# Three unused tiles in front of the split weights, HH and the attention tiles of a two-block float32 kernel

## The chip, the cores and the metric

The kernel runs on one core of a Trainium2 chip. The metric is the device time of one execution in microseconds (us). A profiled execution has a time of its own, from its first to its last instruction, the span.

## The reference

Two blocks act on x of 512 tokens by 1,024 channels, all in float32:

```python
# first block
z = rmsnorm(h, g_mix) @ w_in + b_in                       # 1024 -> 1536
y = concat(conformer_conv_group(a, gate, ...), multiscale_pool_group(p, ...))
h = h + y @ w_out
h = h + (silu(n @ w_gate) * (n @ w_up)) @ w_down          # n = rmsnorm(h, g_ffn); 1024 -> 2816 -> 1024
x = rmsnorm(h, g_final)
# second block: layer 0 has 16 forgetting heads of 64, layer 1 has 8 differential heads
for layer in range(2):
    h = attention(x)                                      # fox, then diff with rope and a shared K, V
    x = layer_norm(ALPHA * x + h)
    f = (silu(g) * val) @ ffn_w_out                       # g, val: x @ ffn_w_in after a causal conv of width 3
    x = layer_norm(ALPHA * x + f)
```

The convolution of the first block is depthwise, 31 taps over 512 channels.

## The kernel before

Every tile has 128 partitions; an activation is held turned, channels on the partitions and the 512 tokens along the row. A float32 product is made of three matmuls on halves of the numbers: each operand is split into a high part in fp32r (XH, WH) and what is left over (XL, WL), and `product` adds WH by XL, WH by XH and WL by XH into one PSUM bank (lines 982 to 984). The weight tile is the stationary operand, 128 by 128; the moving operand is 128 by 512, or by 256 where a stage is worked in halves of the tokens.

The weights come in items of up to 8 tiles. SP's queue copies an item into `raw` (2 slots), ScalarE makes WH of it (line 1604) and GpSimd WL (line 741); WH and WL have 4 slots of 8 tiles of 128 floats each. TensorE waits for a half item's WL (`step`, line 980 and before) and goes through its k tiles. STAGES lists the order of the items: in, out, gu0, down0, qkv1, out1, gu1, down1, qkv2, out2, gu2, down2. The moving operand is XH and XL in the in, gu and qkv stages, HH and HL (the hidden layer, 22 tiles) in the down stages, OH and OL in the out stages after attention. In qkv1 and qkv2 the weight items are woven with the score, softmax and value steps of the heads that came before; those read tiles of the attention group (PTH, PTL, VX, QX, KX and others). The first two items of a stage and the last two are worked in halves of 256 tokens, so that the norm between the stages can overlap them (lines 1055, 1067, 1068, and `half_item`).

The convolution is done on TensorE too: `conv_pairs` (line 1282 on) takes for each pair m of taps 128 weight columns from dg_h and dg_l, and as moving operand 256 floats of u_h and u_l that start at float m. So the moving start goes 4 bytes on with each of the 16 values of m; a row of u_h for one group is 271 floats (1,084 bytes) long, and there are two groups g.

SBUF is laid out by order of allocation. `sb(name, shape, dtype, stack)` takes the next free bytes of every partition, in steps of 32 bytes, and a stack that is closed gives its bytes back, so the tiles allocated next lie over it. From the start of a partition: xres (16,384 bytes); XH and XL (16,384 each), and over them, since `wide` is closed, yout and last_rows; raw (8,192); WH and WL (16,384 each); par (3,072), ones (512), identr (512), masks (1,024), work (12,288), small (432). Then three groups start at the same byte and lie over each other: `first` (xin, upad, dg_h, u_h and more of the first block), `ffn` (HH, HL of 45,056 bytes each, act_g, hid) and `att` (PTH, PTL, OH, OL, OF, pmap, and in it either the tiles of the first or those of the second kind of attention). The functions that use the tiles are the same in both kernels:

```python
            def product(out_, wh, wl, xh, xl, start, stop):
                pe.matmul(out_, wh, xl, start=start, stop=False)
                pe.matmul(out_, wh, xh, start=False, stop=False)
                return pe.matmul(out_, wl, xh, start=False, stop=stop)
```

Of the kernel before, what the change touches and what calls it, by code (L numbers as in the profile page):

```python
# [26 lines left out]
P = 128  # L27
# [170 lines left out]
def two_blocks(nc, A, out):  # L198
    ctx = ExitStack()
    with ctx:  # L200
        def sb(name, shape, dt=F32, stack=None):
            return (stack or ctx).enter_context(nc.sbuf_tensor(name, shape, dt))
# [7 lines left out]
        def sems(name, n):  # L210
# [8 lines left out]
        yout = sb("yout", [P, 2 * QT, S])  # L219
        last_rows = sb("last_rows", [P, DT, S])  # L220
        raw = sb("raw", [P, RAW, DT, P])
        WH = sb("WH", [P, SLOTS, DT, P], F32R)
        WL = sb("WL", [P, SLOTS, DT, P], F32R)
        par = sb("par", [P, 6 * P])
# [39 lines left out]
        icnt = sb("icnt", [P, PAD], stack=first)  # L264
        first.close()
        ffn = ExitStack()
        HH = sb("HH", [P, FT, S], F32R, stack=ffn)
        HL = sb("HL", [P, FT, S], F32R, stack=ffn)
        act_g = sb("act_g", [P, 2, S], stack=ffn)
        hid = sb("hid", [P, 2, S], stack=ffn)  # L270
        ffn.close()
        att = ExitStack()
        PTH = sb("PTH", [P, 2, QT * KEYS + S - P], F32R, stack=att)
        PTL = sb("PTL", [P, 2, QT * KEYS + S - P], F32R, stack=att)
        OH = sb("OH", [P, DT, S], F32R, stack=att)
# [7 lines left out]
        wf, wf_h, wf_l = (x.rearrange("p (k h) -> p k h", h=FOX_HEADS)  # L283
                          for x in (pmap[:, 0, 0:DT * FOX_HEADS], PTH[:, 0, 0:DT * FOX_HEADS], PTL[:, 0, 0:DT * FOX_HEADS]))
        QX = sb("QX", [P, 2, 2, S], F32R, stack=fox)
# [8 lines left out]
        QZ = sb("QZ", [P, 2, 2, S], F32R, stack=dif)  # L294
        KD = PTH[:, 1, 0:2 * S].rearrange("p (c s) -> p c s", c=2)
        QL = PTL[:, 1, 0:S]
# [153 lines left out]
        def down_part(i):  # L450

            t, j = divmod(i, 4)
            sizes = LAST_DOWN if t == DT - 1 else DOWN
            return sum(sizes[:j]), sizes[j]

        def half_of_maps(x, h):

            return x.rearrange("p k (m h c) -> p k m h c", m=2, h=2)[:, :, :, h, :]

        def maps_of_half(x, h):  # L460

            return x.rearrange("p k (h m c) -> p k h m c", h=2, m=2)[:, :, h, :, :]
# [5 lines left out]
        def halves(kt):  # L468

            return slice(0, kt - kt // 2), slice(kt - kt // 2, kt)  # L470
# [9 lines left out]
        def keys_of(x, head, i):  # L480

            return x[:, head, i * P:i * P + (i + 1) * KEYS].rearrange("p (j s) -> p j s", s=KEYS)[:, :, 0:P]
# [245 lines left out]
        def _(pool):  # L728
            own = Chain(pool, gv)

            def low(g, kt=DT, turned=False, of=range(2), count=1):

                s = g.slot(SLOTS)
                for half in of:
                    ks = halves(kt)[half]
                    wl, x, wh = WL[:, s, ks, :], raw[:, g.slot(RAW), ks, :], WH[:, s, ks, :].bitcast(F32)
                    if turned:
                        wl, x, wh = (maps_of_half(WL[:, s], half), half_of_maps(raw[:, g.slot(RAW)], half),
                                     maps_of_half(WH[:, s].bitcast(F32), half))
                    pool.wait_ge(w_hi, g.times(2).n(half + 1) if len(of) == 2 else count)  # L740
# [119 lines left out]
            def lows_of_hidden(name, layer):  # L860
                with pool.Fori(0, FT // 2) as it:
                    for j in range(2):
                        low(Nth(STAGES[name][0] + 2 * j + 3, it, 4))
                        if layer:
# [3 lines left out]
                        pool.tensor_tensor(HL[:, bass.ds(it * 2 + j, 1), :], hid[:, j:j + 1, :],  # L868
                                           HH[:, bass.ds(it * 2 + j, 1), :].bitcast(F32), ALU.subtract).then_inc(h_lo[j], 1)
                        if not layer:  # L870
# [109 lines left out]
        def _(pe):  # L980
# [5 lines that stand above are left out]
            def step(g, b, hi, lo, k0, k, kt, start, stop, turned=False):  # L986
# [3 lines left out]
                if k == kt - kt // 2 and not turned:  # L990
                    pe.wait_ge(w_lo, g.times(2).n(2))
                s = g.slot(SLOTS)
                mm = product(banks[b][:, :], WH[:, s, k, :], WL[:, s, k, :], hi[:, k0 + k, :], lo[:, k0 + k, :],
                             start and k == 0, stop and k == kt - 1)
# [3 lines left out]
            def item(g, b, hi, lo, k0, kt, start, stop):  # L998

                for k in range(kt):  # L1000
                    step(g, b, hi, lo, k0, k, kt, start, stop)
# [29 lines left out]
            def half_item(name, i, b, hi, lo, k0, kt, h, a=0, z=None, first=True, last=True):  # L1031

                g = STAGES[name][0] + i
                c = slice(h * HALF, (h + 1) * HALF)
                s = g % SLOTS
                for k in range(a, kt if z is None else z):
                    if h == 0 and k == 0:
                        pe.wait_ge(w_lo, 2 * g + 1)
                    if h == 0 and k == kt - kt // 2:
                        pe.wait_ge(w_lo, 2 * g + 2)  # L1040
                    mm = product(halves_of[h][b][:, 0:HALF], WH[:, s, k, :], WL[:, s, k, :], hi[:, k0 + k, c], lo[:, k0 + k, c],
                                 first and k == 0, last and k == kt - 1)
                return mm

            def stage_in_halves(name, m):
# [3 lines left out]
                for h in range(2):  # L1049
                    c = slice(h * HALF, (h + 1) * HALF)  # L1050

                    def by_low(k):
                        pe.wait_ge(x_lo, DT + half_tile(m, h, k) + 1)
                        for j in range(2):
                            mm = pe.matmul(bank[(u + j) % 2][:, c], WH[:, (g + j) % SLOTS, k, :], XL[:, k, c],  # L1055
                                           start=False, stop=k == DT - 1)
# [3 lines left out]
                    for k in range(DT):  # L1060
                        pe.wait_ge(x_top, half_tile(m, h, k) + 1)
                        for j in range(2):
# [3 lines left out]
                            s = (g + j) % SLOTS  # L1066
                            pe.matmul(bank[(u + j) % 2][:, c], WH[:, s, k, :], XH[:, k, c], start=k == 0, stop=False)  # L1067
                            pe.matmul(bank[(u + j) % 2][:, c], WL[:, s, k, :], XH[:, k, c], start=False, stop=False)  # L1068
# [27 lines left out]
            def down(name, layer):  # L1096
# [5 lines left out]
                def tile(t, it=0):  # L1102
                    u = Nth(STAGES[name][1] + t, it, 2)
                    bank_free(u)
                    for j in range(4):
                        if t == 0 and j == 3:
                            for q in h_lo:
                                pe.wait_ge(q, (layer + 1) * FT // 2 + OPEN)
                        item(Nth(STAGES[name][0] + 4 * t + j, it, 8), u.slot(2), HH, HL, *down_part(j), j == 0, j == 3)

# [12 lines left out]
                def part(j, h, a=0, z=None):  # L1123
                    i = 4 * (DT - 1) + j
                    return half_item(name, i, 1, HH, HL, *down_part(i), h, a, z, j == 0, j == 3)

# [299 lines left out]
            def attend(e, slot, turn):  # L1426
                pe.wait_ge(o_read[e], turn.n() + OPEN)
                for j in range(QT):
                    mm = product(ob[e][:, j * P:], VH[:, slot, j * P:(j + 1) * P], VL[:, slot, j * P:(j + 1) * P],
                                 *(x[:, e, j * (KEYS + P):j * KEYS + S] for x in (PTH, PTL)), j == 0, j == QT - 1)  # L1430
                mm.then_inc(o_done[e], 1)

            def attend_folded(e, slot, turn):

                pe.wait_ge(o_read[e], turn.n() + OPEN)
                for j in range(QT):
                    v = VX[:, slot, (2 * j + e) * P:(2 * j + e + 1) * P]
                    for x in (PTL, PTH):
                        mm = pe.matmul(ob[e][:, j * P:], v, x[:, e, j * (KEYS + P):j * KEYS + S], start=j == 0 and x is PTL,  # L1439
                                       stop=j == QT - 1 and x is PTH)  # L1440
                mm.then_inc(o_done[e], 1)
# [148 lines left out]
        def _(act):  # L1590
# [226 lines left out]
            def hidden_hi(it, j, name):  # L1817

                act.wait_ge(bank_read[1], Nth(STAGES[name][1] + 2 * j + 1, it, 4).round(2, 1))
                act.activation(HH[:, bass.ds(it * 2 + j, 1), :], hid[:, j:j + 1, :], ACT.Copy).then_inc(h_hi, 1)  # L1820

# [41 lines left out]
            def map_hi(b, used, head, i):  # L1863
                act.wait_ge(t_done[b], used.n(1))
                act.activation(keys_of(PTH, head, i),
                               tb[b][:, 0:(i + 1) * P].rearrange("p (j q) -> p j q", q=P), ACT.Copy).then_inc(pt_h[b], 1)
# [77 lines left out]
            def conv_hidden(name, layer):  # L1944
# [3 lines left out]
                def hidden(it, j):  # L1948
# [14 lines left out]
                    act.wait_ge(hid_ready[j], Nth(FT * (layer - 1) + j, it, 2).round(2, 1) + OPEN)  # L1963
                    act.activation(HH[:, bass.ds(it * 2 + j, 1), :], hid[:, j:j + 1, :], ACT.Copy).then_inc(h_hi, 1)

# [717 lines left out]
```

## Time and profile before

| what | value |
|---|---|
| time, median of 2 runs | 1817.22 us (1816.87 to 1817.57) |
| profiled execution, span | 1818.9 us |
| TensorE busy | 1774.2 us, 98% of the span, 8,755 matmuls |
| GpSimd busy | 1029.9 us, 57% |
| ScalarE busy | 795.8 us, 44% |
| VectorE busy | 765.2 us, 42% |
| granted TensorE clock, mean | 0.991 |

PE is TensorE's matmuls, PEld its weight loads, DVE VectorE, ACT ScalarE, POOL GpSimd. Matmuls are pipelined: a row gives the time that one is in flight, and the next one starts before it ends. The pace of a stretch is therefore read from the starts of its rows, or from the count of matmuls in a window.

### The profile page before, as it was taken

To read this page: it belongs to the slowest core of one execution; us is meant where nothing else is said; L and a number is where in the kernel's file an instruction comes from. 1 tells how busy PE (TensorE), PEld (TensorE's weight loads), DVE (VectorE), ACT (ScalarE), POOL (GpSimd) and SP (SyncE) were. 2 spreads that over 40 slices of the span, in tenths; PEclk is the share of its full clock that TensorE was granted. 3 is DMA by queue.
4 is the path that set the end of the run, shared out by engine and by line. 5 is a ranking of instruction groups with operands and counts; after the bars stand their busy time and mean duration, and the time that the engine had idled before them with its cause. 6 is when DMAs were issued, how large, how long until landed. Compare 5 with 4: busy or idle time off the path is not lost.

```text
span 1818.9 us, 26859 instructions
## 1 busy us (share of the span) xinstructions
PE 1774.2 (98%) x8755; PEld 1477.6 (81%) x8755; DVE 765.2 (42%) x1382; ACT 795.8 (44%) x1674; POOL 1029.9 (57%) x926
## 2 busy tenths in 40 slices
PE   8999999999999999999999999999999999999997
PEld 6879888888887888788888888877777888888886
DVE  7963000001235556553333322487875533333224
ACT  5644323322245555464444422555565644444231
POOL 7856555555462333466666655555554666666551
PEclk9999999999999999999999999999999999999999
DMA  5312333323334454323333233333332233332332
GB/s 153 92 47 82 104 92 92 101 87 103 91 90 115 123 133 122 86 73 99 102 92 94 85 104 87 82 94 81 87 77 79 63 111 93 96 100 78 104 91 97
DMA packets 327253, 171.94 MB, mean 95 GB/s; under 512 B 43459, under 2 KB 316949, under 8 KB 327189
## 3 DMA queue, kind: packets, MB, share of 16 engines
q1 hardware_dynamic: 327172, 171.12, 33.8%
q8 instruction: 35, 0.57, 0.1%
q14 instruction: 30, 0.24, 0.0%
q10 hardware_dynamic: 16, 0.00, 0.0%
HBM read 152.15 MB, written 2.10 MB: 85 GB/s over the span
## 4 chain that ended last, share of the span: by engine, by line
PE 87%; DVE 5%; POOL 3%; ACT 2%; issue 1%; DMA 1%; SPq 0%; DVEq 0%; ACTq 0%; POOLq 0%
PE bank L982 24%; PE bank L984 24%; PE bank L983 24%; PE attended L982 2%; PE attended L983 2%; PE attended L984 2%; PE turned L1423 1%; POOL WL L741 1%; PE attended L1439 1%; PE bank L1055 1%; PE bank L1067 1%; POOL psums L804 1%; PE bank L1068 1%; DVE small L2453 0%; PE score L1406 0%
## 5 line engine op out<-in xcount | busy, mean ns | idle before, releaser
L741 POOL TENSOR_TENSOR WL<-raw,WH 128x512 fp32r<-128x512 f32 (+3 forms) x656 | 774.8, 1203 | 555.6 <-ACT WH L1604 553.1
L982 PE MATMUL bank<-XL,WH 128*128 128x512 f32 x1432 | 568.8, 397 | 3.7 <-DVE work L2576 1.2
L984 PE MATMUL bank<-XH,WL 128*128 128x512 f32 x1432 | 557.8, 390 | 0.0
L983 PE MATMUL bank<-XH,WH 128*128 128x512 f32 x1432 | 557.4, 389 | 0.0
L1604 ACT ACTIVATE WH<-raw 128x512 fp32r<-128x512 f32 (+3 forms) x656 | 338.5, 565 | 307.7 <-PE bank L984 190.9
L984 PEld LDWEIGHTS bank<-XH,WL 128*128 128x128 f32 x1432 | 269.7, 188 | 56.8
L982 PEld LDWEIGHTS bank<-XL,WH 128*128 128x128 f32 x1432 | 270.1, 189 | 55.6 <-DVE work L2576 1.5
L983 PEld LDWEIGHTS bank<-XH,WH 128*128 128x128 f32 x1432 | 270.4, 189 | 49.9
L982 PE MATMUL bank<-HL,WH 128*128 128x512 f32 (+1 forms) x528 | 200.6, 380 | 0.0
L983 PE MATMUL bank<-HH,WH 128*128 128x512 f32 (+1 forms) x528 | 200.3, 379 | 0.0
L984 PE MATMUL bank<-HH,WL 128*128 128x512 f32 (+1 forms) x528 | 200.3, 379 | 0.0
L2365 DVE SCALAR_TENSOR_TENSOR xres<-xres,bank 128x512 f32 (+1 forms) x27 | 18.5, 687 | 260.4 <-PE bank L984 257.7
L868 POOL TENSOR_TENSOR HL<-hid,HH 128x512 f32 x66 | 85.1, 1289 | 70.5 <-ACT HH L1820 70.5
L982 PEld LDWEIGHTS bank<-HL,WH 128*128 128x128 f32 x528 | 98.8, 187 | 21.5
L984 PEld LDWEIGHTS bank<-HH,WL 128*128 128x128 f32 x528 | 98.8, 187 | 21.5
L983 PEld LDWEIGHTS bank<-HH,WH 128*128 128x128 f32 x528 | 98.8, 187 | 21.3
L1860 ACT ACTIVATE pmap<-score,small 128x128 f32<-128x128 f32 (+3 forms) x128 | 67.2, 525 | 102.8 <-DVE small L2453 102.6
L2427 DVE TENSOR_TENSOR hid<-bank,act_g 128x512 f32<-128x512 f32 x21 | 14.5, 692 | 207.5 <-PE bank L984 203.9
L1958 ACT ACTIVATE hid<-bank,par 128x512 f32<-128x512 f32 x42 | 32.7, 778 | 143.6 <-PE bank L984 143.6
L2513 DVE SCALAR_TENSOR_TENSOR hid<-bank,par,hid 128x511 f32<-128x511 f32 x42 | 31.5, 750 | 150.7 <-ACT hid L1958 150.5
L2513 DVE SCALAR_TENSOR_TENSOR act_g<-bank,par,act_g 128x511 f32<-128x511 f32 x42 | 31.5, 750 | 133.8 <-ACT act_g L1958 133.8
L2453 DVE TENSOR_REDUCE small<-score 128x1 f32<-128x128 f32 (+3 forms) x128 | 62.1, 486 | 34.6 <-PE score L1408 23.3
(366 smaller groups left out, 2532.0 us busy)
## 6 DMA issues: line engine op xcount, KB each, us to landing
raw<-in_ffn_w_in SPq DMA_DIRECT2D x88, 512.0 KB, 3.8
raw<-in_w_gate SPq DMA_DIRECT2D x22, 512.0 KB, 3.8
raw<-in_w_up SPq DMA_DIRECT2D x22, 512.0 KB, 3.9
raw<-in_ffn_w_out SPq DMA_DIRECT2D x28, 384.0 KB, 3.3
raw<-in_ffn_w_out SPq DMA_DIRECT2D x28, 320.0 KB, 3.2
raw<-in_a_w_in SPq DMA_DIRECT2D x16, 512.0 KB, 4.2
raw<-in_kv_w SPq DMA_DIRECT2D x32, 256.0 KB, 3.2
raw<-in_w_in SPq DMA_DIRECT2D x12, 512.0 KB, 3.8
```

The source lines that it names most:

```text
L741: pool.tensor_tensor(wl, x, wh, ALU.subtract).then_inc(w_lo, 1)
L804: own.link(pool.tensor_tensor(dst[:, PAD:], src[:, PAD:], src[:, PAD - d:PAD + S - d], ALU.add))
L868: pool.tensor_tensor(HL[:, bass.ds(it * 2 + j, 1), :], hid[:, j:j + 1, :], HH[:, bass.ds(it * 2 + j, 1), :].bitcast(F32), ALU.subtract).th ...
L982: pe.matmul(out_, wh, xl, start=start, stop=False)
L983: pe.matmul(out_, wh, xh, start=False, stop=False)
L984: return pe.matmul(out_, wl, xh, start=False, stop=stop)
L1604: act.activation(wh, x, ACT.Copy).then_inc(w_hi, 1)
L1860: act.activation(pmap[:, n % 4, 0:k], sc[c][:, 0:k], ACT.Exp, bias=small[:, n % 4:n % 4 + 1], accum_out=small[:, 4 + n % 4:5 + n % 4]).the ...
L1958: act.activation(dst[:, j, :], ff_banks(it, j)[side][:, :], ACT.Identity, bias=ff_par(layer - 1, 3, n), scale=ff_par(layer - 1, 2, n)).the ...
L2365: dve.scalar_tensor_tensor(out=r, in0=r, scalar=factor, in1=src[j][:, :].rearrange("p (a s) -> p a s", a=1), op0=ALU.mult, op1=ALU.add).th ...
L2453: dve.tensor_reduce(small[:, n % 4:n % 4 + 1], sc[c][:, 0:(n // 2 + 1) * P], AX_X, ALU.max, negate=True).then_inc(mx[c], 1)
L2513: own.link(dve.scalar_tensor_tensor(out=dst[:, j, 1:], in0=src[:, 0:S - 1], scalar=ff_par(layer - 1, 1, n), in1=dst[:, j, 1:], op0=ALU.mul ...
```

## The change

Three tiles are allocated that nothing reads or writes: 56 floats (224 bytes) in front of WH, 40 floats (160 bytes) at the start of the `ffn` group in front of HH, and 32 floats (128 bytes) at the start of the `att` group in front of PTH. All that is allocated after a gap in the same group moves on by its size; a gap in front of WH moves all three groups as well. The distance from WH and WL, within 128 bytes, is then 32 for XH and XL, 96 for HH and HL and 64 for the attention tiles. No instruction changes but for its addresses.

```diff
         raw = sb("raw", [P, RAW, DT, P])
+        sb("before_w", [P, 56])
         WH = sb("WH", [P, SLOTS, DT, P], F32R)
         WL = sb("WL", [P, SLOTS, DT, P], F32R)
@@
         ffn = ExitStack()
+        sb("before_h", [P, 40], stack=ffn)
         HH = sb("HH", [P, FT, S], F32R, stack=ffn)
@@
         att = ExitStack()
+        sb("before_o", [P, 32], stack=att)
         PTH = sb("PTH", [P, 2, QT * KEYS + S - P], F32R, stack=att)
```

## Rows read from the trace of the kernel before

**Rows 1.** The page, part 1: busy us (share of span), instructions of each engine

```profile
PE 1774.2 (98%) x8755; PEld 1477.6 (81%) x8755; DVE 765.2 (42%) x1382; ACT 795.8 (44%) x1674; POOL 1029.9 (57%) x926
```

**Rows 2.** The page, part 4: the chain that ended last, by engine

```profile
PE 87%; DVE 5%; POOL 3%; ACT 2%; issue 1%; DMA 1%; SPq 0%; DVEq 0%; ACTq 0%; POOLq 0%
```

**Rows 3.** TensorE's timeline (start us, us in flight) where gate/up ends and down begins

```profile
394.18 0.39 PE L984 MATMUL bank<-XH,WL 128*128 128x512 f32 x1
...
398.26 0.39 PE L984 MATMUL bank<-XH,WL 128*128 128x512 f32 x1
398.49 0.39 PE L982 MATMUL bank<-HL,WH 128*128 128x512 f32 x1
```

**Rows 4.** Windows: stretch, its us, PE busy (xmatmuls), clock, DMA share, GB/s

```profile
143.00:149.00 6.00, 6.00 (x52) 1.00 0.31 92
175.00:395.00 220.00, 220.00 (x972) 1.00 0.33 97
400.00:505.00 105.00, 105.00 (x452) 1.00 0.33 96
506.60:516.60 10.00, 10.00 (x90) 1.00 0.49 134
...
1455.00:1675.00 220.00, 220.00 (x972) 1.00 0.33 98
```

**Rows 5.** Early in the kernel: a window (its granted clock 0.50) and TensorE's timeline

```profile
105.30:110.00 4.70, 4.70 (x14) 0.50 0.00 0
...
107.05 0.63 PE L984 MATMUL bank<-XH,WL 128*128 128x512 f32 x1
...
109.61 0.63 PE L984 MATMUL bank<-XH,WL 128*128 128x512 f32 x1
```

**Rows 6.** Timeline of matmuls and weight loads (PEld) in a gate/up stage

```profile
300.11 0.39 PE L983 MATMUL bank<-XH,WH 128*128 128x512 f32 x1
300.12 0.19 PEld L984 LDWEIGHTS bank<-XH,WL 128*128 128x128 f32 x1
```

**Rows 7.** TensorE's timeline in the convolution

```profile
84.94 0.28 PE L982 MATMUL attended<-u_l,dg_h 128*128 128x256 f32 x1
...
87.45 0.28 PE L982 MATMUL attended<-u_l,dg_h 128*128 128x256 f32 x1
...
87.81 0.28 PE L982 MATMUL attended<-u_l,dg_h 128*128 128x256 f32 x1
...
90.19 0.28 PE L984 MATMUL attended<-u_h,dg_l 128*128 128x256 f32 x1
...
91.52 0.28 PE L982 MATMUL attended<-u_l,dg_h 128*128 128x256 f32 x1
91.64 0.28 PE L983 MATMUL attended<-u_h,dg_h 128*128 128x256 f32 x1
...
91.86 0.28 PE L982 MATMUL attended<-u_l,dg_h 128*128 128x256 f32 x1
...
94.38 0.28 PE L982 MATMUL attended<-u_l,dg_h 128*128 128x256 f32 x1
...
94.74 0.28 PE L982 MATMUL attended<-u_l,dg_h 128*128 128x256 f32 x1
```

**Rows 8.** The page, part 5: the costliest group, busy, mean ns, idle before

```profile
L741 POOL TENSOR_TENSOR WL<-raw,WH 128x512 fp32r<-128x512 f32 (+3 forms) x656 | 774.8, 1203 | 555.6 <-ACT WH L1604 553.1
```

**Rows 9.** Groups by line and shape: count, busy us, mean ns of TensorE's matmuls

```profile
L984 PE MATMUL bank<-XH,WL 128*128 128x512 f32 x1416 | 553.3, 391 | 0.0
...
L984 PE MATMUL bank<-HH,WL 128*128 128x512 f32 x462 | 182.0, 394 | 0.0
...
L984 PE MATMUL attended<-HH,WL 128*128 128x256 f32 x66 | 18.3, 277 | 0.0
```

**Rows 10.** TensorE's timeline where a gate/up stage's first whole item begins

```profile
169.98 0.40 PE L982 MATMUL attended<-XL,WH 128*128 128x512 f32 x1
...
171.37 0.39 PE L982 MATMUL attended<-XL,WH 128*128 128x512 f32 x1
```

## The prediction

> **What bounds the kernel now.** I read the page's first part, then the chain that ended last, then the costliest groups, then TensorE's timeline and windows inside single stages. TensorE is busy for 98% of the span and the chain is TensorE for 87% of it [rows 1, 2]; the other engines stand at 42 to 57% [rows 1]. So time is what one matmul's start is after the last one's. The 0.39 us of a row is not that: it is how long a matmul is in flight, and the next starts before it ends. The reader is to look at starts.
>
> In the gate/up stages, where XH and XL are the moving operands, 18 starts lie between 394.18 and 398.26 us: 4.08 / 18 = 226.7 ns [rows 3]. The window of 220 us that holds 972 matmuls, with one or two of them only under way at its edges, says the same: 220 / 970.6 = 226.7 [rows 4]. In the down stage that follows at 398.49 us, with HH and HL moving and the same weight tiles [rows 3], 105 us hold 452: 105 / 450 = 233.3 [rows 4]. TensorE is busy for all of both. With half the columns (256) the order turns round: X takes 6 us for 52 less two, 120 ns; H takes 10 us for 90 less two, 113.6 ns [rows 4]. All four stretches have a granted clock of 1.00, the level of 2.4 GHz. 512 columns at 2.4 GHz are 213.3 ns, so X carries 13.3 ns and H 20 ns more than its columns. At 1.2 GHz, early in the kernel, six X matmuls take 107.05 to 109.61 us, 426.7 ns each, exactly 512 columns at that clock [rows 5]. The extra is thus no fixed cost of an instruction; something that is fast enough at half speed is not at full speed.
>
> What differs between X and H is where they lie. Adding up the allocations, WH, WL, XH and XL all start at a multiple of 128 bytes, and the slices that matmuls take step by multiples of 512; small takes 432 bytes, rounded up to 448, so all that is allocated after it starts 64 past such a multiple. Call d the moving tile's place less the weights', within 128: X has d = 0, H and O have d = 64. While one matmul streams, the weights of the next are loaded: the load of 300.12 us starts 10 ns or less after the matmul of 300.11 [rows 6]. So a relation between the two addresses can matter. The convolution in the first block supports it: its moving tile u_h starts 4 bytes further with each pair of taps, so its 256-column matmuls go through many d. Of the three at d = 64 (91.52 to 91.86 us) the last two take 91.64 to 91.86, 110 ns each within the 10 ns of a row, which is H's figure although here the weights lie 64 bytes off and the moving tile 0; the other half's pairs average (90.19 - 84.94) / 44 = 119.3 ns [rows 7]. So I take it that d counts and not the place of the tile.
>
> **The change, part by part.** No instruction is added or taken away; three unused tiles move addresses. before_w (224 bytes) puts WH and WL 96 past a multiple: X gets d = -96 = 32. before_h (160) gives H d = 64 + 160 = 96. before_o is 128 bytes: the attention tiles keep d = 64.
>
> O: nothing within 128, 0 us. Other engines: their reads and writes of WH, WL, HH and HL move too. WL's subtraction on GpSimd is busy for 774.8 us but GpSimd stands still 43% of the span, most of it (553.1 us) waiting for ScalarE's WH [rows 1, 8]; that idle time covers a few per cent on it. Without that cover, 1% of 774.8 is 8 us. I take 0.
>
> H, 512 columns: 3 x 462 = 1,386 matmuls [rows 9]. The price at d = 96 does not stand in the trace for 512 columns. Bounds: 213.3 ns below (no extra at all: 1,386 x -20.0 = -27.7 us), and above one step more than now, 240.0 (+9.2 us). Why steps: all four settled figures, 226.7, 233.3, 120 and 113.3, are multiples of 6.67 ns, eight cycles of 1.2 GHz, and a stretch that starts between them drifts for some starts and then stays on one (six starts from 169.98 to 171.37 us still take 232 ns each [rows 10], the window that begins at 175 us has 226.7 [rows 4]). For the choice I use the convolution: at d = 96 three of its matmuls take 94.38 to 94.74 us, 120 ns, and at d = 32 three take 87.45 to 87.81, 120 ns as well [rows 7]. That is X's figure for 256 columns, not H's, so I take it that d = 32 and d = 96 behave like d = 0. Then H goes from 233.3 to 226.7: 1,386 x -6.67 = -9.2 us. Its 256-column matmuls, 6 x 66 = 396 [rows 9], go the other way, 113.3 to 120: +2.6 us. H together -6.6 us.
>
> X, 512 columns: 3 x 1,416 = 4,248 matmuls [rows 9]. The stretches of the first and the third gate/up stage hold 972 settled ones each [rows 4], and the second stage has as many items: some 2,900. By the same reading d = 32 behaves like d = 0: 0 us. Bounds: 213.3 ns, 4,248 x -13.3 = -57 us; above, H's present 233.3, +28 us.
>
> Sum: 0 + 0 + 0 - 6.6 + 0. On the profiled span of 1818.9 us this gives 1812.3; the median of the runs is 1817.22, 1.7 us less than the span, so the time is 1810.6.
>
> The Trainium skill speaks against this sum twice. Its page "SBUF — State Buffer", section "Who interferes with whom", has TensorE with two independent read ports, one for the moving operand and one for the weight load, and waiting on nobody; by it an address would change nothing and the time would be 1817.2. By that rule X and H would also cost the same now, and the rows say 226.7 and 233.3; the measurement decides, so its rule gets a chance but not the forecast. Its page "TensorE: Matmul & The Clock Gate", section "Wait — 56ns, not 53.3ns?", gives back-to-back 512-column matmuls 215.7 ns at full clock; an estimate from that page for X and H together would be 4,248 x -11 and 1,386 x -17.6, some 71 us less. The trace has no such stretch with weights loaded for each matmul.
>
> **Rivals.** (1) No effect: d within 128 is not what sets the 226.7 and 233.3. For it: H and X also differ in other address bits. Against: d = 64 in the convolution. 1817.2 us.
> (2) X drops a step, to 220.0: some conflict of the two streams ends when they lie a quarter apart. 4,248 x -6.67 = -28 us, or 2,900 x -6.67 = -19 us if only the settled stretches gain; with H's -6.6, 1782.3 to 1791.3. For it: 220 still is over 213.3, and d = 0, both streams in the same place, looks like the worst layout. Against: no stretch of this trace settles under 226.7, and d = 0 is better than d = 64 today.
> (3) X rises a step, to 233.3, the other side: today d = 0 may be the lucky place and every other one like H or like the drifting starts (232 ns). +19 us for the settled stretches, +28 for all; with H between -6.6 and 0 this is 1830 to 1845. It decides as soon as X rises by more than 6.6 / 4.248 = 1.6 ns in the mean. Two steps would be 1874 at most. For it: the drifting starts, and the attention's mixed stretches that never settle. Against: the convolution's 120 at d = 32.
> (4) H alone gets worse, to 240: +9.2 and up to +2.6: 1829.
>
> **How the numbers follow.** My forecast (X the same, H one step down) 0.36; no effect 0.13; X lower 0.24, of which more than half where it also gains in the mixed stretches or by over a step; X higher 0.22, of which half by more than a step in some stretch; H alone worse 0.05. The 2% that a measurement of this kernel can about tell from no change are 36 us. Faster by over 2% (under 1781) needs all of X a step down and more: 0.17. Slower by over 2% (over 1853) needs X to rise more than one step: 0.11. Within: 0.72. The range runs from 1780 (X one step down everywhere, H too, with 2 us more for the same reason) to 1847 (X one step up everywhere, H unchanged, and 2 us for the X matmuls that rows 9 leave out); the two-step cases are left out.
>
> **What would show it right or wrong.** In the changed kernel's windows the gate/up stretch should hold the same 972 matmuls in 220 us; 1,000 would be rival (2), 943 rival (3). The down stretch of 105 us should hold 463 or so, not 452. The 256-column stretch of H should show 120 instead of 113.3, X's should stay at 120. Attention and out stages should take what they take now. GpSimd's busy time on WL should stay at 775 us. I am wrong if X moves at all, since it has three times as many matmuls as H: the weakest step is to carry a 256-column figure at d = 32 over to 512 columns, when d = 0 and d = 64 change their order between the two.

## The result, and the profile after

The changed kernel takes 1842.03 us (median of 2 runs, 1840.55 to 1843.52) against 1817.22: a ratio of 1.0137, with a 95% interval of 1.0107 to 1.0166. It is slower, by 24.8 us: less than 2%, but the interval leaves no change out. The forecast was 1810.6; the time lies within the range of 1780 to 1847, but on the other side of no change, in rival (3). That the range held is owed to that rival, and not to the mechanism that the forecast was built on.

The first part of the page shows a kernel that does the same work on TensorE over a longer span (before is in [rows 1]):

```profile
span 1838.7 us, 26859 instructions
PE 1795.2 (98%) x8755; PEld 1474.4 (80%) x8755; DVE 764.4 (42%) x1382; ACT 796.1 (43%) x1674; POOL 1033.9 (56%) x926
```

TensorE is busy for 21.0 us more, and the rest of the span, 44.7 us before, is now 43.5: TensorE does not wait more, its stream of matmuls takes longer. The other engines are busy for 4 us more at most. The windows of the changed kernel, to be read against [rows 4] (stretch in us, its length, TensorE busy and its matmuls, granted clock, share of the DMA engines, GB/s):

```profile
141.00:146.00 5.00, 5.00 (x45) 1.00 0.48 134
175.00:395.00 220.00, 220.00 (x945) 1.00 0.32 94
405.00:505.00 100.00, 100.00 (x430) 1.00 0.33 96
511.00:520.00 9.00, 9.00 (x77) 1.00 0.54 148
815.00:1035.00 220.00, 220.00 (x944) 1.00 0.32 95
1475.00:1695.00 220.00, 220.00 (x945) 1.00 0.32 93
```

X in the three gate/up stages: 945 matmuls stand where 972 stood, which is 220 / 943 = 233.3 ns, one step of 6.67 ns up. H: 100 us for 430, less one or two at the edges, again 233.3 ns: nothing gained. The halves of 256 columns moved the other way round: X 5.00 / 43 = 116 ns (120 before), H 9.00 / 75 = 120 ns (113.6 before).

Over the starts of the two traces the mean distance from one matmul to the next is as follows. Distances over 260 ns (512 columns) or 140 ns (256) are left out as waits or as the lower clock; of X's 512-column ones these are 4%.

| moving tile, columns | matmuls with WH or WL | before, ns | after, ns | difference, us |
|---|---|---|---|---|
| X, 512 | 4,512 | 227.4 | 233.3 | +26.6 |
| X, 256 | 576 | 119.2 | 117.1 | -1.2 |
| H, 512 | 1,386 | 233.3 | 233.3 | 0 |
| H, 256 | 396 | 114.5 | 119.8 | +2.1 |
| O, 512 | 288 | 233.2 | 230.5 | -0.8 |
| O, 256 | 192 | 113.6 | 115.6 | +0.4 |

The sum is +27.1 us. The span grew by 19.8 us and the median by 24.8. Part of the difference between span and sum can be the granted clock, which in the profiled execution of before was lower in a few stretches: 0.50 in [rows 5], where the changed kernel has

```profile
105.30:110.00 4.70, 4.04 (x22) 1.00 0.00 0
```

and 0.991 in the mean against 0.996. A mean that is lower by 0.005 is 0.005 x 1,830 = 9 us lost, if TensorE had work in all of those stretches, and less where it had none. So the span should have grown by 18 to 27 us, and did by 19.8; the medians, of two executions each, by 24.8. The sum also takes each mean for all matmuls of its row, the left out ones too.

### The profile page after: what moved, and what is told of

It is laid out like the page before. It is cut to its first block, busy times and chain, and to the rows that moved or that the text cites. A ratio compares the mean times of both kernels' runs of the same rounds, so it can differ in the third digit from the quotient of the medians.

```text
span 1838.7 us, 26859 instructions
## 1 busy us (share of the span) xinstructions
PE 1795.2 (98%) x8755; PEld 1474.4 (80%) x8755; DVE 764.4 (42%) x1382; ACT 796.1 (43%) x1674; POOL 1033.9 (56%) x926
## 4 chain that ended last, share of the span: by engine, by line
PE 87%; DVE 5%; POOL 3%; ACT 3%; issue 1%; DMA 1%; SPq 0%; DVEq 0%; ACTq 0%; POOLq 0%
PE bank L985 24%; PE bank L986 24%; PE bank L987 23%; PE attended L985 2%; PE attended L986 2%; PE attended L987 2%; PE turned L1426 1%; POOL WL L744 1%; PE attended L1442 1%; PE bank L1058 1%; PE bank L1070 1%; POOL psums L807 1%; DVE small L2456 1%; ACT pmap L1863 1%; DVE xres L2167 1%
## 5 line engine op out<-in xcount | busy, mean ns | idle before, releaser
L744 POOL TENSOR_TENSOR WL<-raw,WH 128x512 fp32r<-128x512 f32 (+3 forms) x656 | 778.7, 1210 | 570.5 <-ACT WH L1607 568.1
L985 PE MATMUL bank<-XL,WH 128*128 128x512 f32 x1432 | 575.4, 402 | 3.7 <-DVE work L2579 1.2
L987 PE MATMUL bank<-XH,WL 128*128 128x512 f32 x1432 | 564.4, 394 | 0.0
L986 PE MATMUL bank<-XH,WH 128*128 128x512 f32 x1432 | 564.4, 394 | 0.0
```

The lines of the kernel that those rows point to most:

```text
L744: pool.tensor_tensor(wl, x, wh, ALU.subtract).then_inc(w_lo, 1)
```

## The experiments

Two kinds of kernel were run: the kernel of before with one gap, and a bed in which TensorE works alone from tiles that lie still, with chosen distances between them. Each of the first kind was timed beside the kernel of before on its own chip (1816.20 us in the median of 16 runs on one, 1818.12 of 13 on the other).

Throughout, d is the moving tile's address less the weights', in bytes. Numbers name the rivals of the prediction, letters those of the expectations.

**Only the gap in front of WH.** XH and XL go to d = 32; the groups behind the weights move with them.

```diff
+        sb("before_w", [P, 56])
         WH = sb("WH", [P, SLOTS, DT, P], F32R)
```

> Only the 224 bytes in front of WH: XH and XL go to d = 32, HH, HL and the attention tiles keep d = 64. Theory A: the X stretches go to 233.3 ns as in the changed kernel, H stays at 233.3 for 512 columns and at 113.3 for 256; the time is 1817 + 28 less what the halves of 256 columns give back, 1838 to 1845 us. Rival C (the place of the weights, 96 past a multiple of 128, is what slows the reads): H and the attention stages slow down too, although their d is what it was, to 240 ns: 1850 us or more.

1841.57 us (4 runs) against 1816.20, ratio 1.0140 (1.0123 to 1.0157). This gap alone gives the whole loss. In the windows X has the 945 of the changed kernel; H keeps 100 / 428.6 = 233.3 ns. With 256 columns H takes 116.8 ns over all its starts (7.00 us hold 62), 2.3 more than the 114.5 of before though its distance is the same: that part of the expectation failed.

```profile
175.00:395.00 220.00, 220.00 (x945) 1.00 0.32 94
405.00:505.00 100.00, 100.00 (x430) 1.00 0.33 96
512.00:519.00 7.00, 7.00 (x62) 1.00 0.53 147
```

**Everything moved by 96 bytes.** If the weights' own place were at fault, this would show it.

```diff
+        sb("before_all", [P, 24])
         xres = sb("xres", [P, DT, S])
```

> 96 bytes in front of the very first tile: every address moves by 96, every distance stays. Theory A: each stretch keeps its pace, 1817 us within noise. Rival C: X slows to 233 ns as in the changed kernel, 1840 us or more.

1816.39 us (10 runs) against 1816.20: 0.9995 (0.9986 to 1.0005). 951 matmuls of X in 215 us are 226.7 ns again, and 409 of H in 95 us are 233.3.

```profile
175.00:390.00 215.00, 215.00 (x951) 1.00 0.33 96
405.00:500.00 95.00, 95.00 (x409) 1.00 0.34 98
```

So a shift of all places by 96 bytes changes nothing, while a change of one distance costs 25 us. Rival C falls.

**The bed.** Its core, where w0 moves both tiles and wcols is the number of weight columns; between two stretches stands one matmul of 128 columns from tiles of its own.

```python
            def item(d, w0, cols, wcols):
                e = d // 4 + w0 // 4
                for k in range(DT):
                    w = slice(w0 // 4 + k * P, w0 // 4 + k * P + wcols)
                    x = slice(e + k * S, e + k * S + cols)
                    o = bank[0][0:wcols, 0:cols]
                    pe.matmul(o, WH[:, w], XL[:, x], start=k == 0, stop=False)
                    pe.matmul(o, WH[:, w], XH[:, x], start=False, stop=False)
                    mm = pe.matmul(o, WL[:, w], XH[:, x], start=False, stop=k == DT - 1)
                return mm
```

> TensorE alone, from tiles that lie still; no other engine or queue works beside it. After 192 matmuls of 512 columns at d = 0 come stretches of 144 matmuls at d = 0, 8, 16 and so on to 120, then the same sixteen d with 168 matmuls of 256 columns, then d = 0 with both tiles 32 and 64 bytes on, d = 64 with the weights 32 on, d = 128, 256 and 384, then weight loads of 16 columns at d = 0, 32, 64 and 96, and d = 0 again. It leaves out everything that the reference computes. Theory A (the distance between moving tile and weights within 128 bytes sets the pace, and d = 0 is one of few good places): 226.7 ns at d = 0, 128, 256 and 384 and with both tiles shifted, 233 ns at d = 32, 64 and 96. Rival B (traffic of the other engines or of the DMAs in the same banks makes the extra, and the distance decides when they meet): with all of them silent every stretch runs at one pace near 213 to 216 ns. Rival C (the place of a tile itself counts): d = 0 changes when both tiles are shifted.

Windows of single stretches: d = 0, 8, 16, 32, 64 and 96, then d = 0 with both tiles 32 and 64 bytes on, d = 64 with the weights 32 on, then d = 128, 256 and 384, then d = 0 and 64 with weight loads of 16 columns:

```profile
70.00:98.00 28.00, 28.00 (x125) 1.00 0.00 0
103.00:131.00 28.00, 28.00 (x122) 1.00 0.00 0
136.00:164.00 28.00, 28.00 (x123) 1.00 0.00 0
203.00:231.00 28.00, 28.00 (x121) 1.00 0.00 0
338.00:366.00 28.00, 28.00 (x125) 1.00 0.00 0
472.00:500.00 28.00, 28.00 (x122) 1.00 0.00 0
928.00:956.00 28.00, 28.00 (x125) 1.00 0.00 0
962.00:990.00 28.00, 28.00 (x125) 1.00 0.00 0
995.00:1023.00 28.00, 28.00 (x124) 1.00 0.00 0
1028.00:1056.00 28.00, 28.00 (x122) 1.00 0.00 0
1062.00:1090.00 28.00, 28.00 (x125) 1.00 0.00 0
1095.00:1123.00 28.00, 28.00 (x121) 1.00 0.00 0
1128.00:1156.00 28.00, 28.00 (x123) 1.00 0.00 0
1195.00:1223.00 28.00, 28.00 (x123) 1.00 0.00 1
```

A count is good to one or two: 125 stands for 226.7 ns and once for 228.9 (d = 64), 121 or 122 for 232.4 to 233.4. The means over all starts of each stretch stand in the table below. No DMA moves anything, and the pace at d = 0 and at d = 32 is to 0.1 ns that of X's settled stretches in the two kernels: rival B falls, TensorE makes the extra with its own accesses. The surprise is in the 10th to 12th line, of d = 128, 256 and 384: 256 bytes behave like 0, but 128 and 384 do not (232.4 and 233.4 ns). The description of the change and my prediction both took the distance within 128 bytes; by these figures and the two gaps of 128 bytes below it counts within 256. Within 256, H and the attention tiles stand at d = 192 before (50,624 bytes from WH to HH), not at 64.

> TensorE alone again (it leaves out everything that the reference computes): d = 0, then d = 128 to 248 in steps of 8 with 512 columns, the same with 256 columns, then 4, 12, 252 and 512 with 512 columns, 384 columns at d = 0, 32, 64 and 128, bfloat16 tiles of 512 columns at d = 0, 32, 64 and 128 and of 256 columns at 0, and weight loads of 32, 64 and 96 columns at d = 0. Theory A2 (what counts is the distance within 256 bytes, 0 is the best place for 512 columns): 512 bytes gives 226.7 ns, d = 192 gives the H stages' 233.3 and 113.3 ns, all others 228 to 236. Rival E (a better place than 0 lies in the half that the first bed did not try): one stretch at 220 ns or less. Rival F (the extra over 213.3 ns is the price of a 4-byte operand): bfloat16 runs at 213 to 216 ns at every d; if instead it is a price of loading weights beside any matmul, bfloat16 shows 226 to 233 ns too.

The means, from all starts of a stretch after its first 24, in ns (both beds; d in bytes):

| d | 0 | 8 | 16 | 24 | 32 | 40 | 48 | 56 | 64 | 72 | 80 | 88 | 96 | 104 | 112 | 120 |
|---|---|---|---|---|---|---|---|---|---|---|---|---|---|---|---|---|
| 512 columns | 226.7 | 233.3 | 231.7 | 233.4 | 233.3 | 233.3 | 233.3 | 233.3 | 228.9 | 235.6 | 231.1 | 233.3 | 233.4 | 233.3 | 231.1 | 234.3 |
| 256 columns | 120.0 | 120.0 | 118.7 | 120.0 | 117.8 | 120.0 | 118.3 | 120.0 | 117.8 | 118.3 | 118.3 | 120.0 | 120.0 | 130.1 | 113.3 | 120.0 |

| d | 128 | 136 | 144 | 152 | 160 | 168 | 176 | 184 | 192 | 200 | 208 | 216 | 224 | 232 | 240 | 248 |
|---|---|---|---|---|---|---|---|---|---|---|---|---|---|---|---|---|
| 512 columns | 233.4 | 233.3 | 233.3 | 234.7 | 234.3 | 233.4 | 233.3 | 233.3 | 233.4 | 233.3 | 230.0 | 234.4 | 233.3 | 233.3 | 233.3 | 233.3 |
| 256 columns | 120.0 | 120.0 | 118.7 | 120.0 | 118.7 | 120.0 | 119.3 | 120.0 | 113.3 | 120.0 | 119.1 | 121.3 | 118.3 | 120.0 | 117.1 | 120.0 |

The bed's figures for the stages of the two kernels are in it: X before, at d = 0, 226.7 and 120.0; H before, at d = 192, 233.4 and 113.3; X after, at d = 32, 233.3 and 117.8; H after, at d = 96, 233.4 and 120.0. All eight lie within 1.2 ns of the means in the kernels' table. For 512 columns the natural layout had X on the best figure of all the places tried, and 233.3 is the common price of a place. Rival E falls: nothing in float32r with 512 columns is under 226.7. With 384 columns d = 0 and 64 both take 173.3 ns, d = 128 takes 176.0 and d = 32 176.7: which places are good depends on the width. The next rows are windows at d = 128, at d = 192, then d = 192 with 256 columns, at d = 252, at d = 4, and one of bfloat16 at d = 32:

```profile
75.00:103.00 28.00, 28.00 (x121) 1.00 0.00 0
345.00:373.00 28.00, 28.00 (x121) 1.00 0.00 0
774.00:790.00 16.00, 16.00 (x143) 1.00 0.00 0
1003.00:1031.00 28.00, 28.00 (x125) 1.00 0.00 0
936.00:964.00 28.00, 28.00 (x120) 1.00 0.00 0
1201.00:1228.00 27.00, 27.00 (x126) 1.00 0.00 0
```

bfloat16 tiles take 215.8 ns at d = 32 and 128, with a weight load for each matmul; at d = 0 and 64, where a few records are missing, the starts on record lie 216 apart too. So by the second half of rival F the extra is no price of a weight load beside just any matmul. But the bfloat16 stretch differs in more than the bytes of an operand: its three matmuls take one and the same pair of tiles, and its loads are shorter, 98 ns against 189. These rows show loads of bfloat16 and of float32r in the second bed, and loads of 16 columns in the first (count, busy us, mean ns, idle before):

```profile
L79 PEld LDWEIGHTS bank<-XB,WB 128*128 128x128 bf16 x744 | 72.4, 98 | 69.3
L69 PEld LDWEIGHTS bank<-XL,WH 128*128 128x128 f32 x2120 | 400.4, 189 | 45.4
L63 PEld LDWEIGHTS bank<-XL,WH 128*16 128x16 f32 x192 | 18.2, 95 | 26.1
```

The float32r loads of 16 columns are as short as bfloat16's, and their stretches take 231.1 to 231.7 ns at any of four distances; loads of 32, 64 and 96 columns at d = 0 gave 231.7, 230.0 and 230.0. So a shorter load is not cheaper beside a 512-column stream, it even loses the 226.7, and the length of the load is not what frees bfloat16. That the 4 bytes of the operands do it is the likeliest reading; which of the two operands, no run separates.

**128 bytes in front of WH.** The test in the kernel of 128 against 256.

```diff
+        sb("before_w", [P, 32])
         WH = sb("WH", [P, SLOTS, DT, P], F32R)
```

> 128 bytes in front of WH: within 128 nothing changes, within 256 X goes from 0 to 128 while H and the attention tiles stay at 192. Theory A (the distance within 128 counts): 1816 us as before. Theory A2 (within 256): X of 512 columns goes to about the 232.4 ns of the bed, 3,000 to 4,500 matmuls by +5.7 ns, 17 to 26 us more: 1833 to 1842 us.

1841.24 us (4 runs) against 1818.12: 1.0126 (1.0100 to 1.0152). A gap that by the view "within 128" does nothing costs as much as the change. X stands at 232.8 ns in the mean, H of 512 columns at 233.3 as before, H of 256 at 117.0 as in the run above and not at 114.5:

```profile
175.00:395.00 220.00, 220.00 (x945) 1.00 0.33 97
410.00:505.00 95.00, 95.00 (x409) 1.00 0.33 96
1475.00:1695.00 220.00, 220.00 (x949) 1.00 0.32 94
```

The last line is the third gate/up stage. Its X matmuls take 232.4 ns, those of the first two stages 233.3, with the same tiles at the same distance: they are the two figures that the two beds gave for d = 128.

**128 bytes in front of HH and of PTH.** Within 256, H and O go from 192 to 64.

```diff
+        sb("before_h", [P, 32], stack=ffn)
         HH = sb("HH", [P, FT, S], F32R, stack=ffn)
+        sb("before_o", [P, 32], stack=att)
         PTH = sb("PTH", [P, 2, QT * KEYS + S - P], F32R, stack=att)
```

> 128 bytes in front of HH and of PTH: within 128 nothing changes, within 256 H and the attention tiles go from 192 to 64. Theory A: 1816 us. Theory A2: H of 512 columns from 233.3 to the bed's 228.9 ns, 1,386 x -4.4 = -6.1 us, O -1.2 us, H's 396 of 256 columns from 113.3 or 118 to 117.8, +1 us: 1809 to 1811 us.

1814.24 us (10 runs) against 1818.12: 0.9983 (0.9971 to 0.9996). H of 512 columns goes to 228.9 ns, the bed's figure at d = 64, with 256 columns to 117.8, the bed's again. The paces are those of A2, but the time is over the 1809 to 1811 expected: 3.9 us were gained, not 6. The runs of this kernel had a granted clock of 0.992 in the median against 0.994 beside them, by estimate 0.002 x 1,816 = 3.6 us, which would cover the rest; no run tests that.

```profile
400.00:500.00 100.00, 100.00 (x439) 1.00 0.35 101
```

In the change, the third gap puts the attention tiles at this same d = 64. It was not idle: O of 512 columns stands at 230.0 ns here and went from 233.2 to 230.5 in the changed kernel, and O of 256 columns lost, 113.6 to 115.6.

**X, H and O all at d = 0.** The gap that puts H and O where X is: 192 + 64 = 256.

```diff
+        sb("before_h", [P, 16], stack=ffn)
         HH = sb("HH", [P, FT, S], F32R, stack=ffn)
+        sb("before_o", [P, 16], stack=att)
         PTH = sb("PTH", [P, 2, QT * KEYS + S - P], F32R, stack=att)
```

> Nothing in front of WH; 64 bytes in front of HH and 64 in front of PTH, so that X, H and the attention tiles all have d = 0. Theory A: H of 512 columns goes from 233.3 to 226.7 ns (1,386 matmuls, -9.2 us), its 396 matmuls of 256 columns from 113.3 or 118 to 120 (+1 to +2.6 us), O's 282 of 512 columns -1.9 us: 1807 to 1811 us. Rival D (H is slow for another reason than d, as the number of k tiles in an item or the waits in its stage): no change, 1817 us.

1810.70 us (7 runs) against 1816.20: 0.9972 (0.9961 to 0.9984), 5.5 us faster than before. H takes 226.7 ns (95 us hold 422, where 409 stood in the kernel moved by 96 bytes) and 119.7 with 256 columns, O 228.9. This is the fastest version of the study, and it is the opposite of the change.

```profile
175.00:390.00 215.00, 215.00 (x950) 1.00 0.33 96
405.00:500.00 95.00, 95.00 (x422) 1.00 0.34 99
```

**Which pair of tiles.** The bed once more, with XL or WL moved alone: dh, dl, wh and wl are the bytes by which XH, XL, WH and WL are moved, and at(by, size) is the slice of the k-th tile from there.

```diff
-                    pe.matmul(o, WH[:, w], XL[:, x], start=k == 0, stop=False)
-                    pe.matmul(o, WH[:, w], XH[:, x], start=False, stop=False)
-                    mm = pe.matmul(o, WL[:, w], XH[:, x], start=False, stop=k == DT - 1)
+                    pe.matmul(o, WH[:, at(wh, step)], XL[:, at(dl, S)], start=k == 0, stop=False)
+                    pe.matmul(o, WH[:, at(wh, step)], XH[:, at(dh, S)], start=False, stop=False)
+                    mm = pe.matmul(o, WL[:, at(wl, step)], XH[:, at(dh, S)], start=False, stop=k == DT - 1)
```

> TensorE alone, 512 columns where nothing else is said; it leaves out everything that the reference computes. d = 0; then XL alone moved by 32 to 224 bytes; then WL alone by the same; then all of X by 4, 8, 16, 20, 24, 28 and 228 to 252 bytes; then 256 columns with XL or WL alone moved by 64, 128 and 192; then 512 columns with every weight load from one and the same place, and with loads that step by 128 bytes instead of 512. Theory G (what counts is the distance between a moving tile and the weights that are loaded while it streams): any move of XL alone or WL alone spoils 226.7 ns, to 228 to 234 in the mean, because one or two of the three pairs are then apart; loads from one place keep 226.7; loads that step by 128 bytes alternate between 0 and 128 and cost about the mean of the two, 230. Rival H (the distance between one moving tile and the next counts, and X against W only by accident): moving WL alone leaves 226.7 ns everywhere. Rival E: one of these stretches is under 226 ns, and a faster layout exists.

XL alone on by 32 to 224 bytes gives 228.9 to 232.2 ns, WL alone by the same 231.1 to 233.4. WL alone leaves the moving tiles where they were to each other, so rival H falls: it is a moving tile against weights. Whether against the weights in use or those that are loaded meanwhile, these stretches don't separate. Loads from one place each time keep 226.7; loads that step by 128 bytes, and so alternate between d = 0 and 128, take 231.8, near the 232.4 to 233.4 of d = 128 and not the 230 expected. d = 28 and d = 252 run at 226.7 like 0; d = 4 and 228 at 236.7. d = 240 took 236.7 here and 233.3 in the bed before. The rows are XL on by 32, XL on by 224, WL on by 32, all of X on by 28, and loads from one place:

```profile
70.00:98.00 28.00, 28.00 (x122) 1.00 0.00 0
270.00:298.00 28.00, 28.00 (x123) 1.00 0.00 1
303.00:331.00 28.00, 28.00 (x122) 1.00 0.00 0
706.00:734.00 28.00, 28.00 (x125) 1.00 0.00 0
1078.00:1106.00 28.00, 28.00 (x126) 1.00 0.00 0
```

## Why the prediction was wrong

**What bounds the kernel: right.** TensorE's pace decides, the other engines' tiles could move for nothing, and the third gap was small. The distance counts and not the place: right.

**"d = 32 and d = 96 behave like d = 0": the step that failed.** It came from the convolution's rows of 256 columns. The 256-column part of it held within 3 ns: H went to 119.8 (I said 120), X to 117.1 (I said 120). Carrying it over to 512 columns did not: at d = 32 those take 233.3 ns and not 226.7, at d = 96 233.4. I named this as the weakest step, and it decided the sign: X, forecast at 0, cost +26.6 us, and H of 512 columns, forecast at -9.2, gave 0. The bed shows why 256 columns could not tell: for them d = 0 takes 120.0, as 15 of the 31 other places do, and for 512 columns it is the fast place, 226.7 where 30 of the 31 others take 230.0 or more.

**The modulus: wrong too.** I took over 128 bytes; that H and X differ in other address bits stood in rival (1), and the bit of 128 was one. In the convolution u_h lies 32,768 + 2,176 bytes past dg_h, 128 within 256, and u_l lies at 0. So the pair that I called d = 64 in [rows 7] had u_l at 64 and u_h at 192: the first matmul took 120 ns and the two after it 110 (113.3 is the bed's figure at 192, 117.8 at 64). The row that did not fit, the first of the three, was the evidence, and I left it out of the figure. In the same way the matmuls that I read as d = 32 and d = 96 had u_h at 160 and 224. H before was at 192 and not at 64 as well, so that the two ends I compared, 0 and "64", were 0 and 192, and the attention gap that I priced at nothing moved O: -0.8 us with 512 columns, +0.4 with 256.

**The prior from two points.** With two places seen, one at 226.7 and one at 233.3, I gave a third place the lower figure. The steps misled me too: at most places single distances are no multiples of 6.67 ns, only the sum over a cycle of several matmuls is, so that means such as 228.9 or 231.1 occur and the choice was never between 220.0, 226.7 and 233.3 alone. Rival (3) had the mechanism and its size: X one step up everywhere, +28 us, where +26.6 was measured. The part over the +19 us of the settled stretches is there as well: in the attention stages, woven with the heads' steps, X took 229.2 to 230.4 ns before and 232.8 to 233.6 after (means of stretches of 60 us).

**GpSimd's cover: right.** Its work on WL went from 774.8 to 778.7 us, and TensorE waited no longer for it: its idle time fell by 1.2 us.

The page "SBUF — State Buffer" of the Trainium skill, in "Who interferes with whom", says that TensorE has two read ports, one for the moving operand and one for weight loads, independent of each other, and that it never waits on anyone. For float32r the two are not independent in this case: with every other engine silent, the distance between the two tiles moves the pace from 226.7 to 236.7 ns. For bfloat16 the same bed agrees with the page at the two distances with all records, and its 215.8 ns is the 215.7 that the page "TensorE: Matmul & The Clock Gate" gives in "Wait — 56ns, not 53.3ns?".

What stays open is the mechanism inside: why 16 columns of weights cost as much as 128, which access gives way to which, and why one distance can have two paces. The runs show the map, not the circuit.

## What to carry to other kernels

Where TensorE is the bound and its operands are float32r, the distance between moving tile and weights within 256 bytes was worth 3% of its pace here (226.7 against 233.3 ns). Look at starts, not at the duration of a row, and set the distance to 0 for streams of 512 columns before trying anything else; a tile of odd size in front of a buffer (here `small` with 432 bytes) is enough to lose it. Before pricing a layout from two places, run a bed that sweeps them: the first one, of 1.3 ms, would have told the sign for X, and both together those for H. A figure measured at one width of a matmul need not hold for another.

## What the runs showed of the hardware

- float32r at 2.4 GHz, with a weight load per matmul: 226.7 ns at best for 512 columns, 173.3 for 384, 120.0 for 256 at d = 0, that is 13.3 ns over the columns each time; bfloat16 215.8 and 109.2, 2.5 ns over them. At 1.2 GHz the extra is gone, 426.7 ns for 512 [rows 5].
- The distance counts within 256 bytes: 256 and 512 give 226.7, 128 and 384 give 232.4 to 233.4.
- A steady float32r stream mostly falls into a cycle of one to several matmuls, and the sum of a cycle that repeats is a whole number of 6.67 ns, eight cycles of 1.2 GHz: 226.7 and 233.3 alone; 229 + 232 + 226 at d = 64 (686.7 = 103 x 6.67); 231 + 231 + 238 at d = 96 (700 = 105 x 6.67), which are within 1 ns the distances of H in the changed kernel (231, 232, 237). In some stretches, as at d = 152, no cycle shows within 24 matmuls.
- At one distance two cycles can occur: d = 128 gave 232.4 in one bed and 233.4 in the other, and both in the stages of one kernel; d = 240 gave 233.3 and 236.7; H of 256 columns took 114.5 in the mean before, and 116.8 and 117.0 with the gaps of 224 and 128 bytes in front of WH, at the same distance. So a cell of the table is what one stretch took, to be read with some ns of doubt.
